# Second expert layer of a PEER block: 384 tokens dense, 128 tokens by gathered V rows

## The reference

```python
q = (ht @ w_q).reshape(T, 8, 2, 128)
s = einsum('thpd,hpkd->thpk', q, sub_keys)        # 2 x 128 scores a head
top_s, top_i = top_k(s, 16)                       # 16 + 16 keys a head
cand = top_s[..., 0, :, None] + top_s[..., 1, None, :]
best_s, best_c = top_k(cand.reshape(T, 8, 256), 16)
expert_idx = i1 * 128 + i2                        # i1, i2: first and second key of each choice
gates = softmax(best_s)
act = gelu(einsum('td,thkd->thk', x, expert_u[expert_idx]))
out = einsum('thk,thkd->td', gates * act, expert_v[expert_idx])
```

## Time and profile before

| | us |
|---|---|
| median of three runs | 3117.32 (3115.15 to 3118.13) |
| span of the profiled execution, first to last instruction | 3116.1 |
| TensorE busy in it | 3062.9 |
| first layer with the gates, whole microseconds inside it | 1056 to 1752 |
| second layer, whole microseconds inside it | 1757 to 2466 |

### The profile page before, as it was taken

How to read it: one execution, slowest core, us unless ns; L and a number is a source line. 1 busy time by engine, 2 the same in 40 slices (tenths; PEclk the granted TensorE clock), 3 DMA queues, 4 the chain that set the end, 5 groups by cost and what they waited for, 6 DMA issues and landing times.

```text
span 3116.1 us, 40637 instructions
## 1 busy us (share of the span) xinstructions
PE 3062.9 (98%) x13738; PEld 2470.8 (79%) x13738; DVE 1942.4 (62%) x2787; ACT 715.2 (23%) x1255; POOL 2334.2 (75%) x1127
## 2 busy tenths in 40 slices
PE   7999999999999999999999999999999999899998
PEld 6788877788878888888888888888888775678886
DVE  6488656221253788988876467676767567876621
ACT  3244223220022122121222111111111266332201
POOL 6834654677776888898999888888888762478876
PEclk9999999999999999999999999999999999999999
DMA  4211221223322455444555766666666421122222
GB/s 146 89 54 48 98 75 58 74 94 122 108 95 86 141 186 186 171 157 176 186 182 211 224 188 188 188 188 189 188 188 188 132 75 34 43 91 97 94 94 74
DMA packets 245544, 405.63 MB, mean 130 GB/s; under 512 B 145601, under 2 KB 145729, under 8 KB 244161
## 3 DMA queue, kind: packets, MB, share of 16 engines
q1 hardware_dynamic: 224560, 331.68, 33.9%
...
HBM read 335.04 MB, written 69.21 MB: 130 GB/s over the span
## 4 chain that ended last, share of the span: by engine, by line
PE 93%; DVE 4%; POOL 1%; issue 1%; ACT 1%; DMA 0%; POOLq 0%; SPq 0%; ACTq 0%; DVEq 0%
PE bank L598 20%; PE bank L600 20%; PE bank L599 20%; PE banks L598 6%; PE banks L600 6%; PE banks L599 6%; PE banks L898 2%; PE banks L749 2%; PE banks L711 1%; PE banks L713 1%; PE banks L712 1%; PE banks L814 1%; PE bank L775 1%; PE banks L805 1%; POOL w_lo L506 1%
## 5 line engine op out<-in xcount | busy, mean ns | idle before, releaser
L504 POOL TENSOR_TENSOR w_hi<-w_raw,ones 128x1024 fp32r<-128x1024 f32 x492 | 955.6, 1942 | 713.9 <-PE bank L600 478.5
L506 POOL TENSOR_TENSOR w_lo<-w_raw,w_hi 128x1024 fp32r<-128x1024 f32 x492 | 1232.0, 2504 | 38.6
L598 PE MATMUL bank<-h_hi,w_hi 128*128 128x512 f32 x2000 | 792.3, 396 | 8.1 <-DVE h_lo L1889 7.0
L600 PE MATMUL bank<-h_hi,w_lo 128*128 128x512 f32 x2000 | 780.1, 390 | 0.0
L599 PE MATMUL bank<-h_lo,w_hi 128*128 128x512 f32 x2000 | 778.9, 389 | 0.0
L598 PEld LDWEIGHTS bank<-h_hi,w_hi 128*128 128x128 f32 x2000 | 376.0, 188 | 91.4 <-DVE h_lo L1889 13.9
L600 PEld LDWEIGHTS bank<-h_hi,w_lo 128*128 128x128 f32 x2000 | 375.4, 188 | 80.3
L599 PEld LDWEIGHTS bank<-h_lo,w_hi 128*128 128x128 f32 x2000 | 375.9, 188 | 74.8 <-issue 2.2
L2376 DVE TENSOR_TENSOR ew_lo<-expert_w,ew_hi 128x512 fp32r<-128x512 f32 x128 | 249.3, 1987 | 184.6 <-ACT ew_hi L1593 180.8
L2372 DVE TENSOR_TENSOR expert_w<-acts_in,gates_in 128x512 f32<-128x512 f32 x128 | 243.3, 1937 | 66.4 <-DMA gates_in<-gates 51.6
L2305 DVE TENSOR_TENSOR hot<-bank,tab 128x512 fp32r<-128x512 f32 x256 | 164.5, 684 | 85.0 <-PE banks L898 84.3
...
## 6 DMA issues: line engine op xcount, KB each, us to landing
w_raw<-weights SPq DMA_DIRECT2D x494, 512.0 KB, 3.5
acts<-act_out_stage ACTq DMA_DIRECT2D x128, 256.0 KB, 2.8
gates<-gate_stage ACTq DMA_DIRECT2D x8, 4096.0 KB, 12.9
acts_in<-acts SPq DMA_DIRECT2D x128, 256.0 KB, 4.2
gates_in<-gates SPq DMA_DIRECT2D x128, 256.0 KB, 4.6
resid<-x SPq DMA_DIRECT2D x4, 512.0 KB, 8.3
resid<-x ACTq DMA_DIRECT2D x4, 512.0 KB, 8.2
out<-final SPq DMA_DIRECT2D x3, 512.0 KB, 2.6
```

The source lines that it names most:

```text
L504: nc.gpsimd.tensor_tensor(w_hi[:, pair, :], w_raw[:, slot, :], one_col.to_broadcast((P, 1024)), ALU.mult).then_inc(hi_split, 1)
L506: nc.gpsimd.tensor_tensor(w_lo[:, pair, :], w_raw[:, slot, :], f32(w_hi[:, pair, :]), ALU.subtract).then_inc(split_done, 1)
L598: mm(out_, hi, rhs_hi, start=first, stop=False)
L600: return mm(out_, lo, rhs_hi, start=False, stop=last)
```

## The change

The last 128 tokens leave the dense second layer; the first layer stays dense for all 512.

- **Gates** are made for 384 tokens (`DB = 3` blocks, `DT = 384`), 6 lots in place of 8. `LOT_TILES` has six rows, so 28 U tiles follow the last gates where 8 did.
- **Dense part:** `expert_w`, `ew_hi`, `ew_lo` and all 3072 matmuls work on 384 columns; `acts_in` loads 1.5 KB a partition, `gates_in` 6 runs of 256 B. Both loads of a key count on one semaphore.
- **V split:** ScalarE makes the hi part of a V tile (`value_hi`, 128 x 1024), VectorE the lo part (`value_lo`). `v_hi`, `v_lo` are two more buffers, so four V tiles can be split or in use where two could.
- **Gathered part:** for each of the 128 choices of each of the last 128 tokens (a token a partition) GpSimd gathers the V row from the weights in HBM, in two halves of 512 floats, and the choice's activation from `acts`: 128 x 3 indirect DMAs of 128 descriptors. VectorE computes the indices once (`place_rows`), multiplies activations by gates for 8 choices at a time, and adds each row, times its weight, to `token_sums` (`add_row`, 128 x 1024, both tensors in SBUF). Eight row slots and a list (`sums_of_unit`) spread the 128 sums over units 2 to 61.
- **End:** TensorE turns `token_sums` with eight 128 x 128 transposes into the banks' last 128 columns.
- Some semaphores are shared (`x_part`, `lam_by_act`, `lam_by_dve`); their waits stand where they stood.

```diff
+DB = TT - 1
+DT = DB * P
-LOT_TILES = ((2, 2, 2, 1, 2, 2, 2, 2), (2, 2, 2, 1, 2, 2, 1, 2)) * 3 + ((2, 1, 1, 1, 2, 1, 1, 2), (2, 1, 1, 2, 1, 1, 1, 1))
+LONG, TURNING = (2, 2, 2, 1, 2, 2, 2, 2), (2, 2, 2, 1, 2, 2, 1, 2)
+LOT_TILES = (LONG, TURNING, LONG, TURNING, LONG, LONG)
...
+def sums_of_unit(u):
+    return range(max(u - 2, 0) * CHOICES // (UNITS - 4), min(max(u - 1, 0) * CHOICES // (UNITS - 4), CHOICES))
...
+    def value_slot(n):
+        return (w_hi[:, n % 2, :], w_lo[:, n % 2, :]) if n % RAW > 1 else (v_hi[:, n % 2, :], v_lo[:, n % 2, :])
...
+        def fetch_rows(j):
+            if j >= ROW_SLOTS:
+                pool.wait_ge(row_summed, j - j % 2 - ROW_SLOTS + 2)
+            for half in range(2):
+                pool.indirect_dma_start(
+                    out=row_slot[j % ROW_SLOTS][:, half * 512:half * 512 + 512], out_offset=None, in_=value_rows,
+                    in_offset=bass.IndirectOffsetOnAxis(ap=v_rows[:, half, j:j + 1], axis=0)).then_inc(v_row_in[j // 2 % PAIR_SLOTS], 16)
+        def fetch_acts(n):
+            if n > 1:
+                pool.wait_ge(rows_weighted, n - 1)
+            for j in range(n * CHUNK, n * CHUNK + CHUNK):
+                pool.indirect_dma_start(
+                    out=row_act[:, j:j + 1], out_offset=None, in_=act_words,
+                    in_offset=bass.IndirectOffsetOnAxis(ap=act_row[:, j:j + 1], axis=0)).then_inc(row_act_in[n % 2], 16)
...
-                            ins = three(bank[half * 4 + m][:], w_hi[:, half, col], w_lo[:, half, col],
-                                        ew_hi[:, q * 2 + e, :], ew_lo[:, q * 2 + e, :],
+                            ins = three(bank[half * 4 + m][:, 0:DT], hi[:, col], lo[:, col],
+                                        ew_hi[:, q * 2 + e, 0:DT], ew_lo[:, q * 2 + e, 0:DT],
...
+        def value_hi(n):
+            at = VALUES + n
+            act.wait_ge(raw_loaded[n % RAW], 16 * (at // RAW + 1))
+            act.wait_ge(tile_done, at - RAW + 1)
+            fn(value_slot(n)[0], w_raw[:, n % RAW, :], ACT.Copy).then_inc(v_hi_ready, 1)
...
+        def add_row(j):
+            chunk, rows = j // CHUNK, row_slot[j % ROW_SLOTS]
...
+                tt_(row_w[:, col], row_act[:, col], chosen[:, 3, col], ALU.mult).then_inc(rows_weighted, 1)
...
+            dve.wait_ge(v_row_in[j // 2 % PAIR_SLOTS], 64 * (j // ROW_SLOTS + 1))
...
+                stt(summed[:], rows[:], row_w[:, j:j + 1], summed[:], ALU.mult, ALU.add).then_inc(row_summed, 1)
+        def unit(u):
+            sums = sums_of_unit(u)
+            value_lo(2 * u)
+            if len(sums) > 0:
+                add_row(sums[0])
+            key_lo(2 * u)
+            key_lo(2 * u + 1)
+            value_lo(2 * u + 1)
+            if len(sums) > 2:
+                add_row(sums[1])
+            for key in range(2 * u + 2, min(2 * u + 4, NKEYS)):
+                weigh_key(key)
+            if len(sums) > 1:
+                add_row(sums[-1])
```

More of the change, by code:

```diff
@@ L533, in _ @@
         ahead = 0
[L534 removed]
+        for step in range(DB * LOTS * STEPS):
             n = LOT_TILES[step // STEPS][step % STEPS]
@@ L2380, in sweep_added @@
+        for key in range(2):
+            key_lo(key)
+        for key in range(2, 4):
+            weigh_key(key)
+        dve.wait_ge(split_done, VALUES)
+        value_lo(0)
+        value_lo(1)
+        for u in range(1, UNITS):
+            unit(u)
         def sweep_added(k):
```

235 lines of the change are left out of this document (163 added, 72 removed).

## The result

The changed kernel takes 3079.5 us (median of four runs, 3076.2 to 3089.1) against 3117.7 of the kernel before on the same chip: a ratio of 0.9886, 95% interval 0.9870 to 0.9902. So 38 us are saved where 157 were forecast. The profiled run has a span of 3087.2 us.

The account below looks back on a forecast made before the run. The prediction took TensorE's instruction stream to bound the kernel before, and transfers to bound the changed second layer: 3117.3 - 15.1 - (714 - 570) + 1 = 2959, given as 2960 us; 8-in-10 range 2915 to 3140.

Parts of the forecast that it names:

- The first layer: First layer: 128 gate matmuls of 256 columns leave at 0.118 us each, saving 15.1 us, all on TensorE's path.
- The 384-column step: Second layer's dense matmuls: 0.175 us each in place of 0.2324, so 538 us in place of 714.
- The passes of VectorE and ScalarE: Second layer, per unit of 8.40 us: VectorE needs 7.4 us, ScalarE 3.1 us, so both fit beside TensorE.
- a late gather reaches TensorE by way of `add_row` and `ew_lo`: Second layer: if gathers are late, `add_row` waits, `ew_lo` stands behind it on VectorE, and TensorE waits for that.
- (A): Second layer: transfers become the bound, 4.45 us a key, 570 us for the layer, total 2960; chance 0.37.
- The gather's price: GpSimd, second layer: 1.04 us for each of 384 gathers, 400 us, hidden by TensorE.
- (C): Second layer: the gathers' issue on GpSimd paces it, between 1.37 and 1.88 us each; 3012 at 1.6; chance 0.13.
- Rival (D): Second layer: GpSimd's gathers and VectorE's two-SBUF-input passes shut each other out; slower, 3261; chance 0.22.
- 1.05 as a share that could be held: Second layer's transfers: DMA share taken as held at 1.05, giving 4.45 us a key.
- 74.8 engine-us a key: Second layer's transfers: DMA engine time per key for V tile, activations, gates, gathered rows and gathered activations.
- (B): Second layer: TensorE stays the bound, 538 us plus 2 at the seam, total 2929; chance 0.20.
- the falling clock: Sign of being wrong: waits make TensorE's granted clock fall from 1.00, so every matmul takes longer.

Follow-up runs that it names:

- x3: Changed kernel; after the first eight rows each descriptor of a row's gather brings 16 floats in place of 512, all 384 gathers kept: 3010.7 us.
- x4: Changed kernel; after four keys SyncE loads only 64 columns of each V tile, activations and gates, all 384 gathers at full size: 3000.6 us.
- w5: z1_bunched with a GpSimd memset of 128 x 512 behind every gather: 3021.1 us.
- x2: Changed kernel without the last 112 of 128 activation gathers, so 272 gathers: 2931.6 us.
- z1_bunched: Changed kernel with each row in one gather (256 gathers), GpSimd held until four row slots are free, so gathers come in bunches: 2996.3 us.
- w6_paced_early_acts: Changed kernel with whole-row gathers (256), held to TensorE's finished V tiles, activations fetched eight choices ahead: 2925.6 us.
- z4: Changed kernel with half of the activation gathers after the first 16, so 328 gathers: 3014.8 us.
- z2: Changed kernel with whole-row gathers, plus an unread gather of 16 words behind each row after the eighth (376 gathers): 3088.8 us.
- y4: Changed kernel with 384 gathers, 120 of the activation gathers having 16 descriptors in place of 128: 3074.7 us.
- y2: Changed kernel with all 384 gathers reordered: one activation gather after each row's two, in place of eight before eight rows: 3043.4 us.
- w3: Changed kernel, 384 gathers; each row's two and one activation gather wait until TensorE has finished another V tile: 3028.9 us.
- y3: Changed kernel with all gathers and loads, each sum after the first adding 64 of 1024 columns: 3096.6 us.
- x1: Changed kernel with only the first 32 of 384 gathers; VectorE still adds 128 times from the slots as first filled: 2931.7 us.
- z3: Changed kernel with whole-row gathers (256), one activation gather behind each row, the first ones held by a semaphore: 2945.3 us.

## Why the prediction was wrong, point by point

**Right.** The first layer: the second layer's first matmul starts at 1736.3 in place of 1752.3 (16.0 us against 15.1). The 384-column step: 0.174 to 0.175. The passes of VectorE and ScalarE, to 0.02 us. That a late gather reaches TensorE by way of `add_row` and `ew_lo`: x3, x4 and w5 show this chain alone.

**The step that failed.** The forecast took the gathers as hidden under TensorE, at 1.04 us each, and so made the transfers (A) the bound of the layer, at 570 us. Both halves are wrong. The layer took 698 us, TensorE stood idle for 104 of them on "issue" and lost 56 more in slow matmuls, a term that the sum did not have; and taking 112 gathers away removes this loss, though the DMA share over the layer rises from 0.82 to 0.98 (x2).

**The gather's price.** "128 descriptors are less than a 128 x 512 pass" had no row behind it. A gather starts every 1.25 us at best, and every 1.56 us from 2000 to 2050, beside VectorE's passes. The prediction had worked out that GpSimd paces the layer from 1.37 us on. With 1.56 in the sum the layer comes to 376 x 1.56 + 21 = 608 us, so (C), with 2997, and not (A) would have been the forecast. Its price for 1.6, 3012, is near x3 and x4 (3011 and 3001), not the changed kernel: that has 3079.5, so (C) would have missed the stalls as well.

**VectorE holds the gathers back.** Rival (D) had the two engines shut each other out and charged VectorE for it. It is GpSimd that pays: `add_row`, `ew_lo` and `value_lo` keep the durations forecast for them beside gathers, and the gather waits (0.94 to 3.90 us in the rows of z1_bunched). By the Trainium skill, "SBUF — State Buffer", section "Who interferes with whom", `tensor_tensor` takes only the read interface and does not starve descriptor generation, which it calls inferred. The trace disagrees: the gather at 1816.70 in z1_bunched takes 1.83 us, and nearly all that VectorE does in that time is two `tensor_tensor` passes. A gather also reads its indices from SBUF; whether it is held there or later, no run shows.

**The transfers (A) did not bind.** The working stopped at 1.05 as a share that could be held and at 74.8 engine-us a key. The share measured over 350 us is 1.04, in x2_no_act_gathers (rows in halves, as in the changed kernel) and in w6_paced_early_acts, and TensorE never waits there. So a key takes 1.04 x 16 x 4.20 = 69.9 engine-us, where the prediction has 74.8, or 72.4 without the activations that x2 leaves out: TensorE's pace asks for no more than the 1.05 that the prediction allowed. (B), TensorE as the bound with 2929, is what the same dense work gives once the gathers are fewer: 2925.6 to 2931.7.

**What the working had no term for: the stalls.** The prediction's last sentence had named the falling clock as what would prove it wrong, but as a result of ordinary waits. The runs show what the stalls depend on:

- dense gathers are needed: 272 give none, 328 give 40 us, 376 to 384 give 88 to 99 us (x2, z4, z2, y4, changed kernel), and the order of the 384 matters (39 us in y2, 26 in w3); small ones of 16 descriptors are enough to add (y4, z2). x2 and z4 also differ in kind, since x2 has row gathers alone behind its 32nd; a kernel with 384 row gathers, or a stall that small ones make alone, was not tried;
- full transfers are needed: none with a share of 0.68 or 0.49 over the layer, with just as many gathers (x3, x4);
- neither long `add_row` passes (y3) nor the unrolled lists alone (x1) make them;
- the two conditions are not sharp: x2 has twelve gathers in 15 us at a share of 1.07 without a stall, and four of z1's eight such runs have none;
- once begun, a stall mostly lasts while GpSimd goes on, even with the DMA engines nearly idle (2290 to 2300 us above), and ends when it pauses (2.5 us after the last gather in z3, 1 to 5 us in most cases of the changed kernel).

The last point explains the size, though no run tests it alone. In a stall VectorE stands still, so nothing slows GpSimd, and eight row slots and a chunk of activations ahead let it go on alone: up to 24 gathers, 30 us. Looking ahead, meant to hide the gathers, feeds the stall. w3 fits it: its 384 gathers, interleaved and held to TensorE's pace, leave 26 us of stalls, where y2, interleaved and not held, has 39.

**Open.** Which path is blocked. Engines that wait for no semaphore and get one instruction in 0.7 to 2.1 us look like engines whose instructions or weights are handed over too slowly, but no row here shows that path, and the trace has just 16 instruction packets between 1750 and 2430 us. Why it takes full transfers to begin and none to go on is open as well, and so is why some dense runs beside full transfers pass without harm.
